# One step of a hybrid decoder: x comes transposed from the host and is normalised behind the first products

## The reference

```
xn   = x * rsqrt(mean(x*x) + 1e-6) * g_pre
proj = xn @ w_in                     # columns: qa ka va za | qm km vm om zm | ig fg
att  = sliding-window attention(qa, ka, va) * silu(za)
h    = mLSTM(qm, km/sqrt(128), vm, ig + b, log_sigmoid(fg + b))
m    = sigmoid(om) * rms(h, g_mh) * silu(zm)
y    = x + rms(concat(att, m) @ w_out, g_post)
```

## Time and profile before

| | |
|---|---|
| median of 3 runs | 570.67 us (569.93 to 570.79) |
| the profiled run | 569.42 us, of it 567.6 us in the span of the profile |
| TensorE busy | 548.4 us (97%) |
| VectorE, ScalarE, GpSimd busy | 248.9, 199.9, 135.7 us |
| the chain that ended last | TensorE 74%, VectorE 15%, ScalarE 6%, DMA 2% of the span |
| DMA | 48.72 MB, 86 GB/s in the mean |

### The profile page before, as it was taken

One profiled execution on the slowest core, in us unless ns is written; L12 is line 12 of the kernel. 1 busy time (PEld: TensorE's weight loads), 2 busy tenths in 40 slices (PEclk: granted clock), 3 DMA queues, 4 the chain that ended last, 5 costly groups with the idle time before them and its releaser, 6 DMA issues.

```text
span 567.6 us, 10440 instructions
## 1 busy us (share of the span) xinstructions
PE 548.4 (97%) x4354; PEld 506.7 (89%) x4354; DVE 248.9 (44%) x468; ACT 199.9 (35%) x542; POOL 135.7 (24%) x148
## 2 busy tenths in 40 slices
PE   3999999999999999999999999999999999999996
PEld 2999999999988988889898989899999998888874
DVE  4743214900356565611276767425334327042223
ACT  3342223113254545432565654244322234011011
POOL 3510021112323333431113131245322220011001
PEclk9999999999999999999999999999999999999999
DMA  8431006131142122013233321321123215044321
GB/s 317 146 103 63 1 3 219 70 113 38 38 135 62 63 64 63 24 39 96 74 94 113 91 73 37 100 75 38 39 74 97 90 37 186 0 160 137 108 97 55
DMA packets 34166, 48.72 MB, mean 86 GB/s; under 512 B 3888, under 2 KB 25456, under 8 KB 34104
## 3 DMA queue, kind: packets, MB, share of 16 engines
q1 hardware_dynamic: 25544, 43.80, 23.7%
q10 hardware_dynamic: 8576, 4.26, 2.7%
HBM read 40.48 MB, written 8.56 MB: 86 GB/s over the span
## 4 chain that ended last, share of the span: by engine, by line
PE 74%; DVE 15%; ACT 6%; DMA 2%; issue 1%; POOL 0%; SPq 0%; ACTq 0%; DVEq 0%; POOLq 0%
PE ps L551 36%; PE ps L490 8%; PE ps L492 8%; PE ps L491 8%; ACT prob L954 4%; DVE mx L1239 2%; DVE pT L1254 2%; DVE prob L1227 2%; DVE mx L1240 2%; PE ps L702 2%; PE ps L510 1%; PE ps L714 1%; PE ps L678 1%; PE ps L704 1%; PE ps L495 1%
## 5 line engine op out<-in xcount | busy, mean ns | idle before, releaser
L551 PE MATMUL ps<-x_hl,w_hi 128*128 128x368 f32 (+1 forms) x1200 | 300.0, 330 | 1.3 <-POOL w_lo L329 1.3
L551 PEld LDWEIGHTS ps<-x_hl,w_hi 128*128 128x128 f32 x1200 | 210.2, 188 | 7.9 <-issue 6.4
L551 PE MATMUL ps<-x_hl,w_lo 128*128 128x368 f32 (+1 forms) x600 | 197.1, 329 | 0.0
L551 PEld LDWEIGHTS ps<-x_hl,w_lo 128*128 128x128 f32 x600 | 112.7, 188 | 0.1
L329 POOL TENSOR_TENSOR w_lo<-w_raw,w_hi 128x1024 fp32r<-128x1024 f32 x14 | 33.8, 2415 | 86.0 <-ACT w_hi L864 86.0
L490 PE MATMUL ps<-wt_hi,x_hl 128*128 128x324 f32 x128 | 41.7, 325 | 2.2 <-DVE x_hl L1114 1.5
L954 ACT ACTIVATE prob<-prob,nmx 128x160 f32<-128x160 f32 x64 | 26.7, 417 | 46.6 <-DVE sd L1242 46.6
L492 PE MATMUL ps<-wt_hi,x_hl 128*128 128x324 f32 x128 | 40.5, 316 | 0.0
L491 PE MATMUL ps<-wt_lo,x_hl 128*128 128x324 f32 x128 | 40.4, 316 | 0.0
L1575 POOL TENSOR_TENSOR qmT<-qmT,sg 128x368 f32<-128x368 f32 (+1 forms) x24 | 25.0, 1042 | 57.8 <-DVE sg L1428 36.4
L1525 POOL TENSOR_TENSOR prob<-prob,rden 128x640 f32<-128x640 f32 x16 | 20.1, 1255 | 63.9 <-DVE rden L1248 63.9
(11 more groups left out here) (221 smaller groups left out, 804.9 us busy)
## 6 DMA issues: line engine op xcount, KB each, us to landing
w_raw<-in_w_in_tiles SPq DMA_DIRECT2D x25, 512.0 KB, 3.9
x_raw<-in_x_prompt SPq DMA_DIRECT2D x8, 512.0 KB, 4.4
w_raw<-in_w_out_tiles SPq DMA_DIRECT2D x8, 512.0 KB, 3.2
x_res<-in_x_prompt SPq DMA_DIRECT2D x8, 512.0 KB, 4.4
out_y_prompt<-y_out SPq DMA_DIRECT2D x7, 512.0 KB, 2.9
wt_raw<-in_w_tok SPq DMA_DIRECT2D x4, 648.0 KB, 9.3
Cs<-in_state_C SPq DMA_DIRECT2D x16, 128.0 KB, 2.2
Gt<-r_rows ACTq DMA_DIRECT2D x8, 256.0 KB, 3.5
```

The costliest lines, as they stand in the source:

```text
L551: last = mm(ps[:, 6 + sub % 2, 0:w], wt, xt, start=(at_ == 0), stop=(at_ == 23))
```

## The change

The host now passes x transposed (`x_T`: 8 slices of 128 features by 1088 tokens) and g_pre as columns. The kernel does these things in place of the old token stage:

1. TensorE multiplies a float32 tile of ones by itself 12 times (`idle_x`), into a bank that is overwritten later.
2. Tiles 0 and 1 (ka and the first of qa, six subtiles) come first, k step by k step (`first_tiles`): ScalarE multiplies x by g_pre as it rounds it, VectorE takes the low part, in the place of the raw x. The weights come in slices of 128 rows (`load_first`).
3. ScalarE squares each slice of raw x, VectorE adds the squares up; TensorE sums over features with 9 products by a column of ones (`square_sums`); GpSimd takes the roots; TensorE spreads them over the partitions (`spread_rstd`); VectorE multiplies the six banks by them (`first_evac`).
4. The token tiles are multiplied unscaled, and the scale comes in at the evacuation.
5. Behind each token tile x is put together again, multiplied by the root and split again (GpSimd, VectorE, ScalarE, VectorE; `x_scaled`), for the other tiles.
6. Tiles 2 and 3 are loaded early; `load_w(2)` ahead of `rows_done` is gone, and the loop behind it starts at 4. The row stage starts behind subtile 6, attention at `S_P2` = 17.

The core of the diff:

```diff
-S_P2, S_P3, S_P4 = 3 * FIRST["km"], 3 * FIRST["za"], 3 * FIRST["om"]
+S_KM, S_P3, S_P4 = 3 * FIRST["km"], 3 * FIRST["za"], 3 * FIRST["om"]
+S_P2 = S_KM + 2
+F_TILES = 2
+S_F = 3 * F_TILES
...
-    plan = {-1: [POS[("in", 0)]]}
-    for j in range(NJ - 1):
+    plan = {}
+    for j in range(F_TILES, NJ - 1):
         plan.setdefault(3 * j, []).append(POS[("in", j + 1)])
...
SP
+        for u, (off, w) in enumerate(SUBS):
+            sp.dma_start(xT_raw[:, 0, off:off + w], i["x_T"][:, 0, off:off + w]).then_inc(s(f"x0_ld{u}"), 16)
+        for kk in range(1, KT):
+            sp.dma_start(xT_raw[:, kk, :], i["x_T"][:, kk, :]).then_inc(s(f"x_ld{kk}"), 16)
+            load_first(sp, kk)
...
-        wait(sp, "wt_split_d", 3)
-        wait(sp, "wt_split_p", 3)
-        load_w(0)
-        load_w(1)
+        wait(sp, "w0_lo", KT)
+        load_w(2)
+        load_w(3)
...
-        load_w(2)
         wait(sp, "rows_done", 1)
...
-        for n in range(3, len(SEQ)):
+        for n in range(4, len(SEQ)):
...
TensorE
+        def first_tiles():
+            for kk in range(KT):
+                for pas in range(3):
+                    wt, xt = (w_lo if pas == 1 else w_hi), (xl if pas == 2 else xh)
+                    ...                # waits for w0_hi, w0_lo, xl_ready of this kk
+                    for u, (off, w) in enumerate(SUBS):
+                        ...            # waits for xh_ready
+                        for j in range(F_TILES):
+                            last = mm(ps[:, 3 * j + u, 0:w], wt[:, j, kk * P:(kk + 1) * P], xt[:, kk * T + off:kk * T + off + w],
+                                      start=(kk == 0 and pas == 0), stop=(kk == KT - 1 and pas == 2))
+        def square_sums():
+            wait(pe, "acc_done", KT - 1)
+            for t in range(NTILE):
+                last = mm(ps[0:n, 7, TOK_H + 4 + t:TOK_H + 5 + t], acc[:, off:off + n], ones[:, 0:1], start=True, stop=True)
+        def spread_rstd():
+            wait(pe, "rstd_ready", 1)
+            for t in range(NTILE):
+                last = nc.tensor.transpose(out, stat[0:n, NTILE + t:NTILE + t + 1].broadcast_to([n, P]), ident[0:n, 0:n])
+        def first_token_tile():
+            for q in range(2):
+                if q == 1:
+                    wait(pe, "rstd_act", 1)
+                for kk in range(KT):
+                    if q == 0 and kk == 5:
+                        spread_rstd()
+                    if q == 0:
+                        wait(pe, "wt_split_d", min(kk // 2 + 1, 3))
+                        wait(pe, "wt_split_p", kk // 6)
+                    last = token_products(0, kk, q)
...
+        wait(pe, "idle_ready", 1)
+        for q in range(12):
+            mm(ps[:, 7, 0:P], idle_x[:], idle_x[:], start=True, stop=True)
+        first_tiles()
+        square_sums()
+        first_token_tile()
+        for t in range(1, NTILE):
+            token_major(t)
...
         project(24)
         ...                           # gate transposes, rows_ps
         project(24 * 8)
         wait(pe, "rows_done", 1)
...
ScalarE
+        for kk in range(KT):
+            x_hi(kk)
+            square(kk)
+        for g in range(4):
+            wt_hi_part(g)
+        wait(act, "rstd_ps", 1)
+        A_(rstd_b[:, 0:512], ps[:, 7, :], ACT.Copy).then_inc(s("rstd_act"), 1)
         for t in range(NTILE):
+            token_evac(t)
+            if t == 1:
+                split_hi(2)
+            scaled_hi(t)
VectorE
+        for kk in range(KT):
+            first_hi(kk)
+            x_lo(kk)
+            if kk >= 1:
+                add_squares(kk)
+        wt_lo_part(0)
+        wt_lo_part(1)
+        wt_lo_part(2)
+        mean_squares()
+        first_evac()
+        ...
+        for t in range(NTILE):
+            token_evac(t)
+            x_scale(t)
+            scaled_lo(t)
GpSimd
+        for kk in range(KT):
+            wait(pool, "w0_hi", kk + 1)
+            Q.tensor_tensor(w_lo[:, :, wk], w_raw[:, :, wk], w_hi[:, :, wk].bitcast(F32), ALU.subtract).then_inc(s("w0_lo"), 1)
+        wait(pool, "wt_hi_a", 4)
+        ...                            # low part of the last quarter of the token weights
+        wait(pool, "ms_ready", 1)
+        for r in (stat[:, NTILE:NTILE + NC], stat[0:T_S, NTILE + NC:2 * NTILE]):
+            last = rsqrt(r, r)
+        last.then_inc(s("rstd_ready"), 1)
         for t in range(NTILE):
+            if t == 2:
+                split_lo(pool, Q, 2)
+            wait(pool, "tok_done", t + 1)
+            wait(pool, "x_scaled", t - 1)
+            Q.tensor_tensor(x_sc[:, t % 2, :, 0:n], kx(xh, off, n).bitcast(F32), kx(xl, off, n).bitcast(F32), ALU.add)\
+                .then_inc(s("xsum_ready"), 1)
```

More of the change, by code:

```diff
@@ L522, in token_major @@
             if t == NC:
+                wait(pe, "proj_free", S_F)
                 wait(pe, "xs_ready", 1)
[L524 to L527, removed]
+            for kk in range(KT):
                 for q in range(2):
-                    last = split_products(ps[:, b + q, 0:TOK_H], x_hl[:, :, kk * T + off:kk * T + off + n], x_hl_s[:, kk],
-                                          *(w[:, kk, q * TOK_H:(q + 1) * TOK_H] for w in (wt_hi, wt_lo)),
-                                          first=(kk == 0), final=(kk == KT - 1))
@@ new lines, in x_lo, with add_squares @@
+        def x_lo(kk):
+            x = xT_raw[:, kk, :]
+            wait(dve, "xh_ready", 3 + kk)
+            wait(dve, "sq_ready", kk + 1)
+            STT(out=xl[:, kk * T:(kk + 1) * T], in0=x, scalar=g_col[:, kk:kk + 1], in1=xh[:, kk * T:(kk + 1) * T].bitcast(F32),
+                op0=ALU.mult, op1=ALU.subtract).then_inc(s("xl_ready"), 1)
+        def add_squares(kk):
+            wait(dve, "acc_done", kk - 1)
+            TT(acc[:], acc[:], sq[:, kk % 2, :], ALU.add).then_inc(s("acc_done"), 1)
@@ new lines, in wt_lo_part, with mean_squares @@
+        def wt_lo_part(g):
+            wait(dve, "wt_hi_a", g + 1)
+            r = slice(2 * g, 2 * g + 2)
+            TT(wt_lo[:, r, :], wt_raw[:, r, :], wt_hi[:, r, :].bitcast(F32), ALU.subtract).then_inc(s("wt_split_d"), 1)
+        def mean_squares():
+            wait(dve, "ss_cols", 1)
+            c0 = TOK_H + 4
+            TS(stat[:, NTILE:NTILE + NC], ps[:, 7, c0:c0 + NC], 1.0 / D, EPS, ALU.mult, ALU.add)
+            TS(stat[0:T_S, NTILE + NC:2 * NTILE], ps[0:T_S, 7, c0 + NC:c0 + NTILE], 1.0 / D, EPS, ALU.mult, ALU.add).then_inc(s("ms_ready"), 1)
@@ new lines, in first_evac @@
+        def first_evac():
+            wait(dve, "rstd_ps", 1)
+            CP(rstd_b[:, 512:T_P].rearrange("p (b t) -> p b t", b=4), ps[:, 0:4, 368:368 + P])
+            step(CP(rstd_b[:, T_P:T], ps[:, 4, 368:368 + T_S]))
+            wait(dve, "rstd_act", 1)
+            for sub in (4, 5, 0, 1, 2, 3):
+                j, (off, w) = sub // 3, SUBS[sub % 3]
+                dst = kaT[:, off:off + w] if j == 0 else qaT[:, 0, off:off + w]
+                TT(dst, ps[:, sub, 0:w], rstd_b[:, off:off + w], ALU.mult).then_inc(s("proj_free"), 1)
@@ L1136, in token_evac, with x_scale, scaled_lo @@
+        def x_scale(t):
+            off, n = x_cols(t)
+            x = x_sc[:, t % 2, :, 0:n]
+            wait(dve, "xsum_ready", t + 1)
+            TT(x, x, rstd_b[:, off:off + n].unsqueeze(1).broadcast_to([P, KT, n]), ALU.mult).then_inc(s("xsc_ready"), 1)
+        def scaled_lo(t):
+            off, n = x_cols(t)
+            wait(dve, "xsh_ready", t + 1)
+            TT(kx(xl, off, n), x_sc[:, t % 2, :, 0:n], kx(xh, off, n).bitcast(F32), ALU.subtract).then_inc(s("x_scaled"), 1)
         def token_evac(t):
@@ L1513, in splits @@
                 split_lo(pool, Q, n)
-        for sub in range(S_P2 - 1):
+        for sub in range(S_F, S_P2 - 1):
             splits(sub)
```

277 lines of the change are left out of this document (106 added, 171 removed).

## The result

The changed kernel takes 579.68 us (median of 4 runs, 578.94 to 580.39), the kernel before, run beside it, 570.57 us (569.93 to 570.79). The ratio is 1.0161, its interval 1.0144 to 1.0179: 1.6% slower. The forecast was 575.8 us, the range 570.3 to 581.0. The profiled run took 579.88 us, of it 578.1 us in the span; 572.7 was forecast for the span.

A forecast was written before the change was run, and what follows sets the result against it. TensorE, busy nearly the whole span, was taken as the bound, with the gate rows and weight queue as an even second path. The sum 102.9 + 34.4 + 1.2 + 432.5 + 1.7 gave a 572.7 us span, 575.8 us median; range 570.3 to 581.0.

The forecast's parts named there:

- rival A: The summed forecast, with TensorE stalled 14.5 us for tile 4 behind the row stage: 576 us, chance 0.62.
- rival D: Front goes badly: GpSimd and VectorE hinder each other, warming ends late, root 4 to 5 us late; 580.4 us, chance 0.16.
- Part 1: The start: warming products, not x, set the first real product, at 6.0 us, bounds 5.0 and 7.0.
- Part 2: First six subtiles: 24.1 us of products plus 1.5 us loss as GpSimd slows VectorE, bounds 0 and 4.
- Part 3: Mean square: sums 1.6 us, root transposes 0.9, added wait 2.0 (bounds 0 and 5); token products unchanged at 61.8.
- Part 4: Scaling x again behind the token tiles: a 6 us chain under 7.1 us of products, costed at nothing.
- R: Time the row stage starts, after the front and the gate transposes: forecast 102.9 us.
- Part 5: Tile 4 queued behind the gate rows, usable 34.4 us after the row stage starts; TensorE stands still 14.5 us.
- Behind it: After the tile 4 stall: 432.5 us as before, 1.2 us small transposes and products, 1.7 us cold clock.
- Rival E: Attention ends two subtiles before the next stage instead of four: 2 to 3 us more, 579 us, chance 0.06.
- rival B: The front runs without any wait and the clock stays high after the gap: 568 to 570 us, chance 0.10.
- rival C: Tile 4 doesn't bind, so the 9.8 us and the old 0.6 us are gained: 560 us, chance 0.06.

The follow-up runs named there:

- experiment 3: The changed kernel without the 12 warming products of ones: 580.34 us, ratio 1.0166 against the kernel before.
- experiment 10: The kernel of experiment 8 without the 12 warming products: 565.0 us, ratio 0.9896 against the kernel before.
- experiment 11: The kernel of experiment 8 run once more, unchanged, with the warming products: 564.23 us, ratio 0.9901 against the kernel before.
- experiment 1: The changed kernel with SP issuing weight tile 4 ahead of the wait for the gate rows: 565.9 us, ratio 0.9927 against the kernel before.
- experiment 2: The kernel before, with weight tile 2 issued behind the wait for the gate rows instead of ahead of it: 582.73 us, ratio 1.0217.
- experiment 5: The changed kernel with GpSimd's last quarter of the token weights' low part moved to VectorE: 578.4 us, ratio 1.0135 against the kernel before.
- experiment 6: The changed kernel with GpSimd writing zeros as low parts of weight tiles 0 and 1 instead of subtracting: 578.17 us, ratio 1.0125.
- experiment 7: The changed kernel with tile 4 early, all token-weight low parts on VectorE, mean squares after the second: 564.9 us, ratio 0.9911.
- experiment 8: The kernel of experiment 7 with ScalarE casting the first two tiles' weight slices from the second slice on: 564.36 us, ratio 0.9902.
- experiment 4: The kernel before, with 16 warming products of ones ahead of its first transpose: 569.76 us, ratio 0.9987.
- experiment 9: The kernel of experiment 1 with attention started one subtile sooner: 568.48 us, ratio 0.9967 against the kernel before.

## Why the prediction was right

The sign, the place and the mechanism are those of rival A, the sum. The size is not: the total is 3.9 us over the forecast of 575.8 and outside A's own range of 573 to 579; it lies 0.7 us from the 580.4 of rival D, which has the same stall behind a worse front and had a chance of 0.16. In the spans it is 578.1 against 572.7, 5.4 us. Part by part, in the profile of the changed kernel:

- **Part 1, the first product.** 6.18 us, forecast 6.0. The 24 records of the products of ones took 5.1 us, 0.21 each, near the slow rate that I had taken. (The full rate of the earlier trace rows is 0.13 us a record, not the 0.11 of my text; the sum didn't use it.) What they buy was wrong by kind, though: nothing that experiments 3, 10 and 11 could measure, since VectorE paces the steps.
- **Part 2, the first six subtiles.** They end at 32.4, forecast 31.6 (26.2 us, for 25.6). The loss beside GpSimd was taken at 1.5 us; taking GpSimd's reads away gave 1.9 us back. The lengthening per step was 0.54 us, less than a whole instruction of VectorE's, while GpSimd's subtraction took 1.78 us a step. The Trainium skill ("SBUF — State Buffer", "SBUF: two separate sides") says that the two lock each other out whole; the trace agrees, since GpSimd's subtraction alone takes 0.72 us (at 5.05 in the changed kernel), which bounds what VectorE can lose to it, and the rest of the 1.78 us is less than one instruction of VectorE's.
- **Part 3, the mean square.** This term was undersized, and it is most of the error. Sums 2.04 us (1.6). Then TensorE waits 1.4 us for low weights and 1.2 us for the root, and the nine transposes of the root take 2.27 us (0.9), because the clock has fallen. About 12 products run at the low rate on either side of them (2 us). So the last token product ends at 103.3, forecast 97.9: 5.4 us late, of them 0.2 from Part 1, 0.6 from Part 2, 0.4 from the sums, 4.2 from here. The waits alone, 2.6 us, are near the 2.0 forecast and inside its bounds of 0 and 5. What failed is that I put the clock in this place at nothing: the slow transposes and products make up most of the rest.
- **Part 4, x scaled again.** Hidden, as costed, up to the last tile: the token tiles keep a pace of 7.13 us (7.14 before). At the end VectorE's low part at 103.62 took 2.30 us where the one at 68.98 took 1.24, as GpSimd's next addition ran beside it (103.52, 1.32 us); the gates' transposes began 0.7 us behind the products (a wait of 0.5 in the list) and took 1.21 us for 1.03. R is 109.2, forecast 102.9. It was 112.7 at the same progress before, so only 3.5 us of the 9.8 forecast were gained ahead of the row stage.
- **Part 5, the weights behind the row stage.** Shown, in the new kernel by experiment 1 and in the old by experiment 2. The gap began 19.9 us behind R, as forecast, and ended 32.0 us behind it (34.4): 12.1 us, not 14.5. Of the 2.4 us, 2.1 are in the eight scans, 1.10 us for 3.18, and 0.3 in the transfer of tile 4: the row stage of the earlier trace rows had been slowed by GpSimd, which I carried over as its fixed length.
- **Behind it.** The cold clock cost 2.7 us for 1.7. Rival E came in part: the wait for `ITs` is 1.3 us, 1.0 more than in the kernel of experiment 2, where the mLSTM stage is the old one. Against these 2.0 us, 0.5 was gained elsewhere; where is not shown.

As a sum: +6.3 (R) - 2.4 (row stage and transfer) + 1.5 (behind it) = +5.4 us. R went to 109.2, past rival D's 107.5, in part by D's mechanism (engines in each other's way, a late root) and in part by a low clock in this place that neither A nor D had priced, while the row stage gave part of it back. So two errors of opposite sign made the forecast better than its parts, which is luck. Rivals B and C are refuted: the front has waits, and tile 4 binds.

What stays open is what the last 4 us of the front hang on. Experiments 5 to 8 took its stated causes away one by one, and the time followed by 0.5 to 2 us each; the single profiles show the wait moving from VectorE's low parts to GpSimd's root. The cost of the clock at 38 us was not isolated by an experiment, but the record says more of it than I first read. The seven runs of experiment 1 go from 564.02 to 569.79 us, and their mean granted clock goes the other way: 0.994 to 0.996 in the three of 564 us, 0.992 in the two of 566, 0.988 and 0.986 in those of 568 and 570. The 12 runs of the kernel before beside them keep to 568.92 to 570.93 us. So the new kernel has a cost that changes from run to run at the same program, up to 5.8 us here, and a single profile catches one draw of it. Where in the span the runs without a profile lost their clock is not on record; three profiles of the same front differ just there (last section).

## What to carry to other kernels

When work is pulled ahead of a stage that ends in an in-order queue, ask of each prefetch behind that stage's semaphore how much work the reader has left when the stage ends: six subtiles were pulled to the front and only one more tile (three subtiles) was loaded ahead of the wait, so the cover fell from eight subtiles to five, and one line in SP's queue decided 14 us. A saving on the critical engine is worth nothing in a stretch that another engine paces; here VectorE did, so warming TensorE bought nothing that could be measured. Don't carry a stage's length over from an old profile before looking at what ran beside it. And look at the spread of the runs and their clocks before reading a difference between two single profiles as the effect of an edit.

## What the runs showed of the hardware

**Two engines on one memory, and scans too.** VectorE and GpSimd hold one another up, whoever came first, in these traces about until the other's instruction has ended. The first of VectorE's low parts in the changed kernel took 4.24 us beside GpSimd's 3.30, the others 1.50. In experiment 6 it was GpSimd's, 6.49 us for 3.30. GpSimd's two power instructions took 2.17, 3.38 and 4.79 us as none, one or two VectorE subtractions ran beside them. The running maxima of the mLSTM's decode tokens, eight scans of 8 elements on 4 partitions, are caught by it as well. Chain of waits and GpSimd's timeline of the kernel before:

```profile
106.86 3.18 DVE row L1196 x8
```

```profile
106.26 2.79 POOL L329 TENSOR_TENSOR w_lo<-w_raw,w_hi 128x1024 fp32r<-128x1024 f32 x1 [14.72 <-ACT w_hi L864]
```

One of the eight took 2.28 us and the median one 0.21: the long one ends when GpSimd's subtraction does, at 109.05. All 13 profiles agree. In the eight in which GpSimd splits a weight tile at that time (the kernel before and experiments 1, 4 and 7 to 11) the scans take 3.17 to 3.19 us; in the five in which it does nothing then (the changed kernel and experiments 2, 3, 5 and 6) they take 1.10.

**The clock fell without a long idle gap, and not at the same time in each run.** From 32.4 to 37.7 us of the changed kernel's profile TensorE had 18 one-column records, waits of 1.2 and 0.3 us and a few products, busy for 3.87 of 5.30 us, and at 37.7 its clock was at 0.50. Experiments 1 and 9 have the same front, word for word. By the spacing of the products the low level lasts from 37.6 to 44.4 us in the changed kernel, from 36.0 to 39.3 in experiment 9, and until 47.9 in experiment 1. Timeline and window of experiment 9, for the 2.27 us and the clock of 0.50 of the changed kernel:

```profile
40.81 1.28 PE L531 MATMUL ps<-ident,stat 128*128 128x128 f32 x9 [1.15 <-POOL stat L1530]
```

```profile
37.70:43.00 5.30, 4.15 (x23) 3.64 (x23) 1.64 (x6) 0.60 (x1) 2.17 (x2) 0.85 0.02 3
```

Both profiles reach the sums at 32.4 us, and the row stage starts at 107.6 us in experiment 9 and at 109.2 in the changed kernel: the longer low stretch, 3.5 us more at half the rate, accounts for about these 1.6 us. Whether the one-column products or the short waits let the clock fall was not isolated.

**The way back** costs 2.7 us behind the gap of 12.1 us and 1.5 us behind that of 11.6 us, one profile each.
